# Three-pass products ordered by kind of pass, and decode pages issued from two queues

## What is computed

```
def swiglu(h, wg, wu, wd):
    return (jax.nn.silu(h @ wg) * (h @ wu)) @ wd
...
        h = modulate(x, P['norm_pre'][layer, 0], mod[:, 0, 0], mod[:, 0, 1])
        y = swiglu(h, P['ffn_wg'][layer, 0], P['ffn_wu'][layer, 0], P['ffn_wd'][layer, 0])
        x = gated_residual(x, y, P['norm_post'][layer, 0], mod[:, 0, 2], MACARON_W)
...
            y, hg_s, ssm_s, conv_s = mixer_ab(h, layer, hg_s, ssm_s, conv_s, P)
...
            y, ckv, kpe = mixer_mla(h, pos0, past_ckv, past_kpe, P)
...
    past_ckv = cache_ckv[page_table].reshape(db, -1, MLA_KV_RANK)
    past_kpe = cache_kpe[page_table].reshape(db, -1, MLA_ROPE)
```

## Time and profile before

| | |
|---|---|
| median of 3 runs | 3391.02 us (3389.15 to 3396.61) |
| the profiled execution | 3391.65 us, its span 3390.1 us |
| granted TensorE clock, mean | 0.927 of full speed |
| PE busy | 3042.2 us (90%) |
| PEld busy | 2446.8 us (72%) |
| DVE, ACT, POOL busy | 1379.6, 1322.7, 40.5 us |
| read from HBM | 333.01 MB, mean 102 GB/s over the span |

### The profile page before, as it was taken

How to read it: one execution, slowest core, us unless ns; L and a number is a source line. 1 busy time by engine, 2 the same in 40 slices (tenths; PEclk the granted TensorE clock), 3 DMA queues, 4 the chain that set the end, 5 groups by cost and what they waited for, 6 DMA issues and landing times.

```text
span 3390.1 us, 56102 instructions
## 1 busy us (share of the span) xinstructions
PE 3042.2 (90%) x22503; PEld 2446.8 (72%) x22503; DVE 1379.6 (41%) x2522; ACT 1322.7 (39%) x1774; POOL 40.5 (1%) x74
## 2 busy tenths in 40 slices
PE   6999978999899988999999999988999468999997
PEld 3887867888688766888777887765566346778875
DVE  3343247787455644443234432223322113344322
ACT  3554345555222244554335543322222113355432
POOL 0000000000000000000000000000000000000000
PEclk7999989999888888999999999989999677999998
DMA  5223431221112133223422234311110684322221
GB/s 215 87 96 114 171 122 63 76 76 69 60 66 102 53 139 118 75 96 118 153 105 75 99 110 153 142 72 40 37 37 0 190 244 174 136 75 98 91 86 59
DMA packets 57047, 346.67 MB, mean 102 GB/s; under 512 B 7345, under 2 KB 7682, under 8 KB 27266
## 3 DMA queue, kind: packets, MB, share of 16 engines
q1 hardware_dynamic: 51122, 318.66, 26.8%
q0 software_dynamic: 5840, 26.83, 2.2%
HBM read 333.01 MB, written 12.45 MB: 102 GB/s over the span
## 4 chain that ended last, share of the span: by engine, by line
PE 81%; DVE 7%; SPq 4%; ACT 3%; issue 2%; DVEq 2%; DMA 1%; ACTq 0%; POOL 0%; PEldq 0%
PE PS L757 19%; PE PS L756 18%; PE PS L758 16%; PE PS L738 9%; PE PS L770 2%; PE PS L898 2%; SPq L659 2%; SPq L661 2%; PE PS L1094 1%; PE PS L1095 1%; PE PS L794 1%; PE PS L1107 1%; PE PS L1074 1%; PE PS L1082 1%; PE PS L861 1%
## 5 line engine op out<-in xcount | busy, mean ns | idle before, releaser
L756 PE MATMUL PS<-hid_hi,w_hi 128*128 128x260 f32 x2816 | 1012.2, 367 | 33.5 <-DVE hid_rest L1603 33.1
L757 PE MATMUL PS<-hid_rest,w_bf 128*128 128x260 bf16 x2816 | 805.9, 286 | 0.0
L1567 DVE TENSOR_TENSOR w_rest<-weight_ring,w_hi 128x1024 bf16<-128x1024 f32 (+1 forms) x304 | 363.6, 1197 | 1046.8 <-ACT w_hi L1252 1046.7
L758 PE MATMUL PS<-hid_bf,w_rest 128*128 128x260 bf16 x2816 | 775.3, 275 | 0.0
L1251 ACT ACTIVATE w_bf<-weight_ring 128x1024 bf16<-128x1024 f32 (+1 forms) x304 | 314.3, 1034 | 957.8 <-PE PS L758 955.7
L756 PEld LDWEIGHTS PS<-hid_hi,w_hi 128*128 128x128 f32 x2816 | 538.3, 191 | 80.9 <-issue 44.2
L756 PE MATMUL PS<-gu_hi,w_hi 128*128 128x260 f32 x1408 | 507.4, 368 | 5.6 <-DVEq L502 5.6
L757 PE MATMUL PS<-gu_rest,w_bf 128*128 128x260 bf16 x1408 | 403.4, 286 | 0.0
L758 PE MATMUL PS<-gu_bf,w_rest 128*128 128x260 bf16 x1408 | 387.9, 275 | 0.0
L757 PEld LDWEIGHTS PS<-hid_rest,w_bf 128*128 128x128 bf16 x2816 | 271.0, 96 | 114.5
L1252 ACT ACTIVATE w_hi<-weight_ring 128x1024 fp32r<-128x1024 f32 (+1 forms) x304 | 309.8, 1019 | 0.0
(11 more groups left out here) (370 smaller groups left out, 4203.3 us busy)
## 6 DMA issues: line engine op xcount, KB each, us to landing
weight_ring<-in_ffn_gu SPq DMA_DIRECT2D x88, 1024.0 KB, 4.8
ada_chunks<-in_ada_w SPq DMA_DIRECT2D x40, 1536.0 KB, 6.4
weight_ring<-in_ffn_wd SPq DMA_DIRECT2D x32, 1408.0 KB, 6.0
arena<-in_pages SPq DMA_DIRECT2D x72, 288.0 KB, 3.2
weight_ring<-in_w_hgrn SPq DMA_DIRECT2D x16, 1024.0 KB, 4.9
weight_ring<-in_ada_w SPq DMA_DIRECT2D x8, 1536.0 KB, 7.0
weight_ring<-in_w_ssm SPq DMA_DIRECT2D x8, 1536.0 KB, 6.5
weight_ring<-in_mla_pairs SPq DMA_DIRECT2D x8, 1536.0 KB, 6.2
```

Of the source, the lines that this page charges most:

```text
L756: pe.matmul(out, w_hi[:, buf, cols], hi[:, first + k, half], start=start and k == 0, stop=False)
L757: pe.matmul(out, w_bf[:, buf, cols], rest[:, first + k, half], start=False, stop=False)
L758: last = pe.matmul(out, w_rest[:, buf, cols], bf[:, first + k, half], start=False, stop=stop and k == n - 1)
L1567: tt(WL_[:, buf, 0:n], W[:, slot, j * DC * P:j * DC * P + n], WH[:, buf, 0:n].bitcast(F32), ALU.subtract).then_inc(w_rest_ready, 1)
```

## The change

The order of the passes is turned round. In `product_by_pass` all tiles of a group go through the hi pass (16 matmuls for eight tiles), then all through the bf pass, then all through the rest pass. PE waits for `w_hi_ready` ahead of the first and for `w_rest_ready` only ahead of the third. Where the input comes tile by tile (`product_by_tile`: 4 groups of the up products, 4 of the output projections), each tile does both halves of a pass before the next pass, and the waits stay as they were. In the recurrence, `sums()` of QUERY moves from the middle of the product to behind its hi pass. In decode, SP issues the even pages and GpSimd the odd ones, each counting its own semaphore, and PE waits for both.

```
-            def product_of_parts(bank, buf, n, first, hi, bf, rest, start, stop, before=None,
-                                 weights=None):
+            def product_by_tile(bank, buf, n, first, hi, bf, rest, start, stop, before):
...
+                for k in range(n):
...
+                    before(k)
+                    for w, x in ((WH, hi), (WB, rest), (WL_, bf)):
+                        for hf in range(2):
+                            last = pe.matmul(PS[:, bank + hf, 0:HT], w[:, buf, cols],
...
+            def product_by_pass(g, bank, buf, n, first, hi, bf, rest, start, stop, weights=None, between=None):
+
+                w_hi, w_bf, w_rest = weights or (WH, WB, WL_)
+                pe.wait_ge(w_hi_ready, g + 1)
+                for w, x in ((w_hi, hi), (w_bf, rest), (w_rest, bf)):
+                    if w is w_bf and between:
+                        between()
+                    if w is w_rest:
+                        pe.wait_ge(w_rest_ready, g + 1)
+                    for k in range(n):
+                        for hf in range(2):
+                            last = pe.matmul(PS[:, bank + hf, 0:HT], w[:, buf, k * P:(k + 1) * P],
+                                             x[:, first + k, hf * HT:(hf + 1) * HT],
+                                             start=start and w is w_hi and k == 0,
+                                             stop=stop and w is w_rest and k == n - 1)
                 return last
...
-                        project(h + 1, QUERY, 0, lambda k: sums() if k == DC // 2 else None)
+                        project(h + 1, QUERY, 0, sums)
...
-                            for pg in range(NPAGE):
+                            for pg in range(0, NPAGE, 2):
...
+            with pool.Fori(0, NB // 2) as b:
+                for bb in range(2):
+                    pool.wait_ge(k_free[bb], b + 1)
+                    for pg in range(1, NPAGE, 2):
+                        page = pool.value_load(TABLE[0:1, bass.ds(b * (2 * NPAGE) + (bb * NPAGE + pg), 1)],
+                                               min_val=0, max_val=A["pages"].shape[0] - 1)
+                        pool.dma_start(PAGES[bb][pg], A["pages"][page]).then_inc(k_in_odd[bb], 16)
...
-                    pe.wait_ge(k_in[bb], b2 * (16 * NPAGE) + 16 * NPAGE)
+                    pe.wait_ge(k_in[bb], b2 * (8 * NPAGE) + 8 * NPAGE)
+                    pe.wait_ge(k_in_odd[bb], b2 * (8 * NPAGE) + 8 * NPAGE)
```

More of the change, by code:

```diff
@@ L478, in build_program @@
         k_free = [sem("k_free0"), sem("k_free1")]
+        k_in_odd = [sem("k_in_odd0"), sem("k_in_odd1")]
         b_q = sem("b_q")
@@ L743, in tiles @@
                 return [W[:, slot, (first + k) * P:(first + k + 1) * P] for k in range(n)]
-            def product_of_parts(bank, buf, n, first, hi, bf, rest, start, stop, before=None,
-                                 weights=None):
-                w_hi, w_bf, w_rest = weights or (WH, WB, WL_)
+            def product_by_tile(bank, buf, n, first, hi, bf, rest, start, stop, before):
                 for k in range(n):
                     cols = slice(k * P, (k + 1) * P)
-                    if before:
-                        before(k)
-                    for hf in range(2):
-                        out = PS[:, bank + hf, 0:HT]
-                        half = slice(hf * HT, (hf + 1) * HT)
-                        pe.matmul(out, w_hi[:, buf, cols], hi[:, first + k, half], start=start and k == 0, stop=False)
-                        pe.matmul(out, w_bf[:, buf, cols], rest[:, first + k, half], start=False, stop=False)
-                        last = pe.matmul(out, w_rest[:, buf, cols], bf[:, first + k, half], start=False,
-                                         stop=stop and k == n - 1)
+                    before(k)
[3 more added lines that the diff above has]
+                                             x[:, first + k, hf * HT:(hf + 1) * HT],
+                                             start=start and w is WH and k == 0,
+                                             stop=stop and w is WL_ and k == n - 1)
+                return last
@@ L812, in step @@
                         g, buf = group(("up", s), i, jj, j)
-                        pe.wait_ge(w_rest_ready, g + 1)
-                        product_of_parts(4 * jj + 2 * j, buf, DC, 0, HH, HB, HL, True, True,
-                                         before if j == 0 else None).then_inc(part_done, 1)
+                        if before and j == 0:
+                            pe.wait_ge(w_rest_ready, g + 1)
+                            product_by_tile(4 * jj + 2 * j, buf, DC, 0, HH, HB, HL, True, True, before)\
+                                .then_inc(part_done, 1)
+                        else:
+                            product_by_pass(g, 4 * jj + 2 * j, buf, DC, 0, HH, HB, HL, True, True)\
+                                .then_inc(part_done, 1)
                 step(0, 0, normed)
@@ L840, in step @@
                         g, buf = group(stage, i, jj, j)
-                        pe.wait_ge(w_rest_ready, g + 1)
-                        product_of_parts(2 * jj, buf, tiles_in(stage, j), j * DC, *parts, j == 0, j == groups - 1,
-                                         (lambda k: before(j * DC + k)) if before else None).then_inc(part_done, 1)
+                        if before:
+                            pe.wait_ge(w_rest_ready, g + 1)
+                            product_by_tile(2 * jj, buf, tiles_in(stage, j), j * DC, *parts, j == 0, j == groups - 1,
+                                            lambda k: before(j * DC + k)).then_inc(part_done, 1)
+                        else:
+                            product_by_pass(g, 2 * jj, buf, tiles_in(stage, j), j * DC, *parts, j == 0,
+                                            j == groups - 1).then_inc(part_done, 1)
                     if s < 5:
@@ L865, in hgrn, with project @@
             def hgrn():
-                def project(h, c, bank, before=None):
-                    g = hgrn_group(h, c)
-                    pe.wait_ge(w_rest_ready, g + 1)
-                    product_of_parts(bank, c % 2, DC, 0, GHH, GHB, GHL, True, True, before, (GWH, GWB, GWL))\
-                        .then_inc(part_done, 1)
+                def project(h, c, bank, between=None):
+                    product_by_pass(hgrn_group(h, c), bank, c % 2, DC, 0, GHH, GHB, GHL, True, True,
+                                    (GWH, GWB, GWL), between).then_inc(part_done, 1)
                 def head(h, more):
```

1 line of the change is left out of this document (added).

## The result

| | before | after |
|---|---|---|
| median | 3391.22 us (3389.15 to 3396.61) | 3313.04 us (3312.54 to 3314.85) |
| span of the profiled execution | 3390.1 us | 3313.3 us |
| granted TensorE clock, mean | 0.927 | 0.928 |

The ratio is 0.9768, with a 95% interval of 0.9751 to 0.9785: the change makes the kernel 78 us faster, 2.3%. The forecast was 3257 us, 134 us faster. The direction was right and the size was off by 56 us. In the profiled executions 76.8 us are gained.

A forecast was written before the change was run, and what follows sets the result against it. PE's pace through three-pass triples was taken to set more than half the time, page issue to bound decode. Passes 105.8, recurrence 9 and decode 20 sum to 134.8 us; 3391.65 less that gives 3257; range 3240 to 3275, 8-in-10 range 3240 to 3340.

The forecast's parts named there:

- rival 2: Grouped passes: a hi step costs 124 ns, as a switch does now; 188 ns less a group of eight, 3313 us; chance 0.13.
- The 418 ns: Forecast range: saving per group if every step took 111 ns, 15 us more in total than the forecast.
- The pace of the triples: Three-pass products on PE: 358.5 ns a triple, 5.74 us a group of eight, sets more than half the time.
- A hi step takes 112 ns: Grouped hi pass: hi to hi step of 112 ns, 368 ns less a group of eight, 105.8 us outside the recurrence.
- the other 247: Old triple of 358 ns: what the steps hi to bf and bf to hi share, some 124 ns each.
- Rival 1: Hi pass: a float32r stream holds off the next float32r load, 225 ns a step; 3796 us, slower; chance 0.15.
- its sign of 0.12 to 0.13 us: Changed profile: hi loads starting 0.12 to 0.13 us apart would show rival 2.
- The recurrence, 9 us: Recurrence: `h_done` about 1.0 us earlier and 0.3 at ACT's copy, 1.2 to 1.3 us a head, 9 us in all.
- Decode, 20 us: Decode, odd pages on GpSimd: sequences 16.8 us apart instead of 19.4, set by full DMA engines; 20 us less.
- rival 4: Decode: GpSimd too slow; at 2.6 us a page no gain, at 3.5 us 35 us later, 3312 us; chance 0.03.
- My floor of 15.2 us: Decode: a sequence's period if PE alone set it, from its start to L1155's end; would gain 32 us.
- Rivals 3: Rival 3, grouped passes: a hi step costs 136 ns, the order gives nothing, only decode gains; 3371 us; chance 0.05.

The follow-up runs named there:

- value_cut_later: Changed kernel; in the recurrence ACT takes a head's first exponential before cutting VALUE's weights, DVE the levels' differences before VALUE's rest: 3305.22 us, ratio 0.9750.
- pages_only: The kernel before, old order of passes, with decode's odd pages issued by GpSimd: 3377.95 us, ratio 0.9957.
- three_bf16: Changed kernel with the later VALUE cut and three bfloat16 passes, rests taken against bfloat16 values, no float32r copies: 3243.57 us, ratio 0.9559.

## Why the prediction was right or wrong

**The number.** 3313 lies outside the forecast's own range of 3240 to 3275. It lies inside 3240 to 3340 since I had widened that to take in rival 2, and not through the mechanism that I forecast. (The 418 ns behind that range is 408 by its own steps, 5736 − 48 × 111, and the 15 us are 12.)

**The pace of the triples (right).** 5.74 us a group and PE as what sets it were as I read them. PE has gone through the groups by pass outside the recurrence without idle time before them, but for 5.6 us in the down products behind DVE, as many as before, and the cuts still hide.

**"A hi step takes 112 ns" (the step that failed).** It takes 120.8. My two rows for it were float32 loads in a row, and showed how closely loads follow each other; neither had a float32r stream of 260 columns beside it. I let the load decide and took the stream to be that of any 260 columns. The wrong turn was one step earlier: I gave the whole excess in "the other 247" to the switches, where only their sum was in the rows. My ends in hundredths of a microsecond even had the two steps the other way round, 0.13 us into the hi pass and 0.12 out of it. Over the whole trace they are 120 and 127 ns, and 120 is what a float32r stream takes wherever it stands. Read from end to end, before's own trace had this number: the rest to hi step ended 120 ns on, though a hi load hides. Only the 127, by its 14 or 15 ns over a bf step, is a switch's.

With the measured steps a group of eight is 15 × 120.8 + 31 × 112 + 247 = 5531 ns, so 205 less and not 368; a group of six some 150 less. 264 × 0.205 + 32 × 0.150 = 58.9 us, and the stages show 61.0, for which I had 105.8. Of the 47 between, 15 × 8.8 × 264 + 11 × 8.8 × 32 = 38 us are the hi steps and the rest is bf's 112 in place of 111.

**Rival 1 (wrong), the held-off load.** Loads of the hi pass start with the matmul before, and the step is 120 ns and not 225. The Trainium skill (TensorE: Matmul & The Clock Gate, The mechanism) states that weight loads overlap matmuls in flight only where the row groups differ; the prediction names another section of that page for it. This trace does not bear it out: all loads of the passes take all 128 rows, they start during the matmul before, and steps are 112 and 120 ns.

**Rival 2 (its mechanism was the case).** Of its two causes the load was not it, the other was: it named the float32r stream as a part of the 247, with hi steps of 124 ns, and its sign of 0.12 to 0.13 us is the one that came. Its total of 3313 is the measured one in part by accident: the passes gave 61.0 us where it had 54.0, the recurrence and decode some 10 less than it had. I gave it 0.13 for want of a row against it, and took the nearer-looking row as the forecast.

**The recurrence, 9 us (wrong).** I counted 1.0 us a head for `h_done` and 0.3 for the copy. `h_done` did come 0.71 earlier, and the copy had its 0.3. But ACT's chain starts from QUERY's end, which comes only 0.22 earlier, and it, not GATE's start, leads to the copy. I had read ACT's idle time at the copy and not what ACT does between QUERY's end and there. What was left, 0.35 us in the head followed above, went in two heads to a longer stretch at the lower clock. That the cut's place on ACT is the bound is shown by `value_cut_later`: ACT then waits for PE, and long parts at the same granted clock are 0.7 us shorter.

**Decode, 20 us (right in kind, 4 to 5 too many).** GpSimd takes 1.24 us a page where I put 1.5, so rival 4, which needed 2.6, was out. The first sequence still waits 19.0 us (23.35 before): both queues have issued its pages some 9.3 us after they start, and the rest is transfer, with landings up from 3.2 to 5.9 us. The period is 17.3, where I had 16.8 from full DMA engines. The number is near, the reason was not: the DMA engines stand at 0.79, and from the second on each sequence waits for DVE's L1986 and no page. So the sequence's own chain through PE, ACT and DVE sets it, and by that more queues would give nothing; no run tried them. My floor of 15.2 us for this chain left out its end, the 1.1 to 1.3 us from the turned result to the next sequence's start. The rest goes with the clock: where the granted clock from start to start is 0.80 or 0.81 a period takes 16.2 to 16.6 us, and where it is 0.70 or 0.71 it takes 16.9 to 17.5, in after and `pages_only` alike. `pages_only` has three such short periods of its seven and after one, beside a first one of 18.5 us at 0.67.

The Trainium skill (DMA: Bandwidth & Descriptors, Issuing engines are not separate DMA queues) says that only the time to issue is saved by a second issuing engine. That agrees with these runs: issue was what the stage waited for, and `pages_only` gains 15.0 us.

**Rivals 3 and 4 (wrong).** The passes alone give 59.5 us, and the pages alone 15.0.

## What to carry to other kernels

Before a step that has no row is priced by its neighbours, ask which of its two halves, load or stream, each neighbour holds fixed; a sum over two unlike steps must be split by their ends in the trace before one of them is used for something new. When the order of matmuls is changed, only the switches are won back; the price of the operand's type stays in each column. Changing the order gave 60 us here, and changing the hi pass's type 46 on top. When PE's work in a chain with ACT and DVE gets shorter, look for what stands on ACT between the two PE products, and move what nobody waits for behind what somebody does.

## What the runs showed of the hardware

- A float32r stream takes 0.45 ns a column at granted clock 1.00 (120 ns for 260, 117 for 256, 234 for 512), a bfloat16 stream of 260 columns 111 to 112 ns. Neither a weight load of 135 ns in place of 188 nor a second half from column 256 makes it shorter.
- A float32 load of 188 ns hides wholly beside a float32r stream of 120: at 135 ns the step is the same. A bfloat16 load behind a float32r stream starts only near that stream's end, and that step takes 127 ns by the modelled ends. A triple with its two switches takes 14 ns more than its three streams.
- A page read from the table and sent by GpSimd takes it 1.24 us, about as much as SP's 1.2. With two queues a page's way from issue to landing nearly doubles, 3.2 to 5.9 us, while the rate rises from 244 to 280 GB/s.
- The granted clock of a head's long part was 0.95 in each of the six before, and 0.90, 0.95 or 1.00 in kernels whose gaps on PE differ by a microsecond or two. Between 0.95 and 1.00 lie 0.6 to 0.9 us in `value_cut_later` and 1.6 in `three_bf16`, between 0.90 and 0.95 some 1.4 in after and 1.6 in `three_bf16`. What makes the stretch at the lower level long in one head and short in the next stays open; I had no run that sets it.
